# Moving the low-part splits of the weight units from GpSimd to VectorE, in the pairs stage of a two-block model kernel

## The reference, cut to what matters

```
r, k, v = split(conv3x3(h @ w_in[:, :3072]))             # context stream: 3-tap conv
w_log   = a_w0 + tanh(lora_w) @ a_w2;   iclr = sigmoid(a_a0 + lora_a @ a_a2)
decay   = exp(-exp(-softplus(-w_log) - 0.5))
kk      = k * a_k_k * rsqrt(sum_head((k * a_k_k)^2))
S <- S diag(decay) + (S a) b^T + v k^T,  y = S r         # per head, over tokens, both directions
```

## Time and profile before

| | |
|---|---|
| device time, 3 runs | 2478.40, 2481.42 (median), 2490.73 us |
| span of the profiled execution, first to last instruction | 2477.4 us (4.0 us under the median of the runs; its own time around the span is not given apart) |
| PE busy | 2412.3 us, 97% |
| DVE busy | 1255.9 us, 51% |
| ACT busy | 1190.7 us, 48% |
| POOL busy | 1353.1 us, 55%, nearly all in L171 |
| pairs stage | from about 170 to 888 us, some 85 us a pair |

### The profile page before, as it was taken

How to read it: one execution, slowest core, us unless ns; L and a number is a source line. 1 busy time by engine, 2 the same in 40 slices (tenths; PEclk the granted TensorE clock), 3 DMA queues, 4 the chain that set the end, 5 groups by cost and what they waited for, 6 DMA issues and landing times.

```text
span 2477.4 us, 60217 instructions
## 1 busy us (share of the span) xinstructions
PE 2412.3 (97%) x23314; PEld 2018.9 (81%) x23314; DVE 1255.9 (51%) x2368; ACT 1190.7 (48%) x1899; POOL 1353.1 (55%) x571
## 2 busy tenths in 40 slices
PE   6999999999999999999999999999999999999997
PEld 2278778777877878889999988888888888888886
DVE  5637776776677333245655445455344443333322
ACT  6533443444344334444444455555665555555554
POOL 0033211231122134437888887878777877777785
PEclk9989999999999999999999999999999999999999
DMA  8831211120111123326676654555455555555553
GB/s 344 309 109 62 70 47 48 56 70 30 56 62 64 47 78 102 100 97 212 236 254 236 238 186 165 175 170 176 164 167 173 186 169 178 169 178 169 170 181 133
DMA packets 100150, 361.40 MB, mean 146 GB/s; under 512 B 11120, under 2 KB 14320, under 8 KB 99728
## 3 DMA queue, kind: packets, MB, share of 16 engines
q1 hardware_dynamic: 99072, 357.90, 42.6%
q10 hardware_dynamic: 912, 1.03, 0.2%
HBM read 356.79 MB, written 2.10 MB: 145 GB/s over the span
## 4 chain that ended last, share of the span: by engine, by line
PE 93%; DVE 3%; ACT 2%; issue 1%; DMA 1%; SPq 0%; DVEq 0%; ACTq 0%
PE ps L207 26%; PE ps L208 13%; PE ps L180 6%; PE ps L181 6%; PE ps L182 6%; PE ps L633 6%; PE ps L634 4%; PE ps L635 4%; PE ps L813 2%; PE ps L803 1%; PE ps L827 1%; PE ps L881 1%; DMA W<-stream 1%; PE ps L848 1%; PE ps L711 1%
## 5 line engine op out<-in xcount | busy, mean ns | idle before, releaser
L171 POOL TENSOR_TENSOR wlo<-raw,whi 128x1024 fp32r<-128x1024 f32 x563 | 1349.6, 2411 | 1105.0 <-ACT whi L161 1066.4
L207 PE MATMUL ps<-acts,whi 128*128 128x512 f32 x2560 | 912.0, 401 | 1.4 <-DVE acts L2606 1.4
L161 ACT ACTIVATE whi<-raw 128x1024 fp32r<-128x1024 f32 x566 | 596.0, 1054 | 320.7 <-PE ps L208 136.7
L208 PE MATMUL ps<-acts,wlo 128*128 128x256 f32 x2560 | 714.9, 279 | 0.0
L207 PEld LDWEIGHTS ps<-acts,whi 128*128 128x128 f32 x2560 | 480.8, 188 | 114.0 <-DVE acts L2606 1.7
L208 PEld LDWEIGHTS ps<-acts,wlo 128*128 128x128 f32 x2560 | 482.6, 189 | 0.9
L180 PE MATMUL ps<-acts,whi 128*128 128x256 f32 (+1 forms) x1088 | 328.0, 301 | 0.0
L182 PE MATMUL ps<-acts,wlo 128*128 128x256 f32 (+1 forms) x1088 | 324.8, 299 | 0.0
L181 PE MATMUL ps<-acts,whi 128*128 128x256 f32 (+1 forms) x1088 | 324.8, 298 | 0.0
L633 PE MATMUL ps<-acts,whi 128*128 128x512 f32 (+1 forms) x576 | 224.0, 389 | 0.9 <-DVE W L1425 0.9
L180 PEld LDWEIGHTS ps<-acts,whi 128*128 128x128 f32 x1088 | 208.0, 191 | 8.3 <-POOL wlo L171 1.5
(11 more groups left out here) (361 smaller groups left out, 3343.4 us busy)
## 6 DMA issues: line engine op xcount, KB each, us to landing
raw<-stream SPq DMA_DIRECT2D x566, 512.0 KB, 3.3
W<-stream SPq DMA_DIRECT2D x64, 512.0 KB, 4.7
graw<-stream SPq DMA_DIRECT2D x32, 512.0 KB, 4.6
W<-xT SPq DMA_DIRECT2D x1, 4096.0 KB, 17.8
XR<-xT SPq DMA_DIRECT2D x16, 128.0 KB, 5.1
outT<-XR SPq DMA_DIRECT2D x4, 512.0 KB, 3.3
cns<-consts SPq DMA_DIRECT2D x1, 1056.0 KB, 5.1
cns<-consts SPq DMA_DIRECT2D x1, 896.0 KB, 7.3
```

Of the source, the lines that this page charges most:

```text
L161: nc.scalar.activation(whi[slot], raw[slot], ACT.Copy).then_inc(hi_done, 1)
L171: nc.gpsimd.tensor_tensor(wlo[slot], raw[slot], whi[slot].bitcast(F32), ALU.subtract).then_inc(lo_done, 1)
L207: nc.tensor.matmul(both_parts, whi[slot][:, k, :], hl[:, :, k0 + k, :], start=first and k == 0, stop=False)
L208: ins = nc.tensor.matmul(ps[:, bank, 0:T], wlo[slot][:, k, :], hl[:, 0, k0 + k, :], start=False, stop=last and k == UK - 1)
```

## The change

POOL's loop in the pairs stage goes; POOL only waits until the 67 units are done. In its place DVE has `dve_lo(dve, j, n)`, the same subtraction on the same tiles, at fixed places of its own list. Each of them first waits until ACT has made the high part (`hi_done`) and the ring place is free (`unit_used`). In a regular pair, units 5, 6, 7 stand in the scan, units 0, 1, 2 of the pair after it in the later part of the same scan, unit 3 in level 2 of the inverse and unit 4 at its end. At the start, DVE waits for POOL's last unit, then takes (0,3), (0,4), (0,5) ahead of `dve_decay(0)`, (0,6) ahead of the k convolution, (0,7) ahead of the r convolution and (1,0) ahead of `dve_norm_k(0)`; (1,1) and (1,2) stand ahead of `dve_rho(0)` in pair 0's inverse.

```diff
--- before.py
+++ after.py
@@ -1153,9 +1153,14 @@
             nc.gpsimd.memset(padk, 0.0).then_inc(R["pad_zero"].sem, 1)
             nc.gpsimd.memset(padr, 0.0).then_inc(R["pad_zero"].sem, 1)
             nc.gpsimd.memset(padc, 0.0).then_inc(R["pad_zero"].sem, 1)
-            with pool.Fori(0, PAIRS) as i:
-                for k in range(U_PAIR):
-                    split_lo(pool, (S_PAIR + k + LEAD) % RING, (i, U_PAIR, S_PAIR + k + LEAD))
+            pool.wait_ge(lo_done, pair_unit(PAIRS, LEAD))
+
+        def dve_lo(dve, j, n):
+
+            s = pair_unit(j, n)
+            dve.wait_ge(hi_done, s + 1)
+            dve.wait_ge(unit_used, s - (RING - 1))
+            nc.vector.tensor_tensor(wlo[s % RING], raw[s % RING], whi[s % RING].bitcast(F32), ALU.subtract).then_inc(lo_done, 1)
 
         def eight(v):
 
@@ -1368,6 +1373,8 @@
             if i:
                 dve_ydev(dve, i - 1)
             else:
+                dve_lo(dve, 1, 1)
+                dve_lo(dve, 1, 2)
                 dve_rho(dve, 0)
                 R["rho_ok"].wait(dve, 1)
                 R["dec_ok"].wait(dve, 3)
@@ -1391,6 +1398,8 @@
                         queried(0)
                     elif lv == 3:
                         go(conv_v, 2)
+                if lv == 2 and i + 1 < PAIRS:
+                    dve_lo(dve, i + 1, 3)
                 if lv == 4:
                     go(conv_v, 3)
                 elif lv == LEVELS:
@@ -1423,6 +1432,8 @@
                         dve_half(dve, i + 1)
             R["bonus_mm"].wait(dve, i + 1)
             nc.vector.tensor_tensor(bonp, ps[:, 0, 0:T], vc[:, 0:T], ALU.mult).then_inc(R["bonp_ok"].sem, 1)
+            if i + 1 < PAIRS:
+                dve_lo(dve, i + 1, 4)
 
         def dve_scan(dve, i):
 
@@ -1447,7 +1458,9 @@
             dve_keys(dve, j)
             state(1)
             dve_decay(dve, j)
+            dve_lo(dve, j, 5)
             state(2)
+            dve_lo(dve, j, 6)
             go(conv_r, 7)
             state(3)
             go(conv_r, 2)
@@ -1457,12 +1470,16 @@
             state(4)
             dve_keyed(dve, j)
             dve_keyed_ways(dve, j)
+            dve_lo(dve, j, 7)
             state(5)
             dve_alpha(dve, j)
             dve_scaled_keys(dve, j)
+            dve_lo(dve, j + 1, 0)
             state(6)
             dve_rho(dve, j)
             dve_bonus_in(dve, j)
+            dve_lo(dve, j + 1, 1)
+            dve_lo(dve, j + 1, 2)
             return conv_v
 
         def dve_pairs(dve):
@@ -1470,10 +1487,17 @@
             nc.vector.memset(kst_[:, 1:2], LN_EPS).then_inc(R["kconst"].sem, 1)
             nc.vector.memset(kst_[:, 2:3], 1.0).then_inc(R["kconst"].sem, 1)
             dve_half(dve, 0)
+            dve.wait_ge(lo_done, pair_unit(0, LEAD))
+            dve_lo(dve, 0, 3)
+            dve_lo(dve, 0, 4)
+            dve_lo(dve, 0, 5)
             dve_decay(dve, 0)
+            dve_lo(dve, 0, 6)
             go(dve_conv_k(dve, 0), 13)
             dve_keys(dve, 0)
+            dve_lo(dve, 0, 7)
             go(dve_conv_r(dve, 0), 10)
+            dve_lo(dve, 1, 0)
             dve_norm_k(dve, 0)
             dve_alpha(dve, 0)
             dve_beta(dve, 0)
```

## The result

| | kernel before | changed kernel |
|---|---|---|
| device time, median of 20 runs | 2482.93 us (2478.40 to 2490.73) | 2488.80 us (2483.63 to 2493.38) |
| ratio to before, 95% interval | 1 | 1.0025 [1.0017, 1.0033] |
| span of the profiled execution | 2477.4 us | 2486.8 us |
| DVE busy | 1255.9 us | 1233.7 us |
| POOL busy | 1353.1 us | 1199.4 us |

The change makes the kernel 5.9 us slower, 0.25%; forecast were 3.8 us and 2485.2 us. In a second comparison the same kernel came out at 1.0040 [1.0027, 1.0053]. So the loss is real and small.

The account below looks back on a forecast made before the run. PE was taken to bound the kernel, DVE having time to spare. Regular pairs -1.3, start +2.7 and inverse +2.4 summed to +3.8 us; on the median of 2481.4 that gave 2485.2 us, range 2476 to 2493.

Parts of the forecast that it names:

- What bounds: Pairs stage: PE sets the pace, busy 89.3 of 90 us; DVE's work costs time only where PE waits for it.
- Regular pairs, -1.3 us: Scans: DVE's stalls behind POOL go, so six PE gaps of 0.53 us become 0.31; the new subtractions cost nothing.
- third rival: PE's unexplained pauses amid small matmuls, 4.6 us together, fall into the new waits or go: 2480.6 us, chance 0.18.
- The start, +2.7 us: Pair 0's start: subtraction ahead of the decay delays ACT 4.45 us, PE waits 2.6, first square comes 2.7 us later.
- The inverse, +2.4 us: Pair 0's inverse: two subtractions ahead of dve_rho delay the key mask; PE's second half of the keys comes 2.4 us later.
- The clock: Second rival: PE's new waits near 190, 211 and 222 us lower its clock; one fall gives 2492 us, chance 0.07.
- signs of being wrong: Late state or L1404 each pair, clock 0.50 after 170 us, first square before 211, or pairs shorter by over 0.3 us.
- thin stretch of rows 10: Kernel before: PE busy 1.1 of 3.7 us, then granted clock 0.50 for 13.7 us; each new gap was called shorter.
- The 4.0 us that the prediction put between span and median: Whole kernel: the runs' median was taken to lie 4.0 us above the profiled span of 2477.4, at 2481.4 us.
- A late subtraction in every pair: First rival: subtractions at the two narrow places come late in each of 7 pairs, 17 us, 2502 us, chance 0.10.
- the narrow place: Unit 5 behind dve_decay in the scan: a 1.21 us subtraction put into a 1.32 us wait, 0.1 to spare.
- a clearly faster kernel: Fourth rival: DVE's stalls set PE's pace after all in the regular pairs; 17 us less, 2464 us, chance 0.05.

Follow-up runs that it names:

- e7: Changed kernel with every DVE subtraction from unit 3 of pair 1 on made twice; 1.0040 of the kernel before.
- e2: Only the start of the change: DVE subtracts up to unit 2 of pair 1, POOL the rest as before; 1.0036 of the kernel before.
- e9: The reordered start of e3, with POOL subtracting from unit 3 of pair 1 on as in the kernel before; 0.9981 of the kernel before.
- e1: Only the regular part of the change: POOL subtracts up to unit 2 of pair 1, DVE from unit 3 on; 1.0008 of the kernel before.
- e3: Changed kernel with the subtractions of the start and of pair 0's inverse moved to where DVE would wait anyway; 0.9989 of the kernel before.
- e4: Changed kernel with 5, 4 and 4 unused matmuls on PE ahead of pad_k, first square and key mask waits in pair 0; 1.0015 of the kernel before.
- e5: Changed kernel with only the part ahead of pair 0's inverse reordered as in e3; 1.0004 of the kernel before.
- e6: Changed kernel with only pair 0's inverse reordered as in e3; 1.0013 of the kernel before.
- e8: Changed kernel with 2 unused matmuls on PE in each of the three waits of pair 0; 1.0013 of the kernel before.
- e10: The changed kernel once more, unaltered, on the chip of e9; 1.0040 of the kernel before.

## Why the prediction was right, and where it was not

**What bounds.** That PE sets the pace in the regular pairs held: e7 adds 9.7 us of DVE to each pair for 0.4 us, its clock fall included.

**Regular pairs, -1.3 us.** The mechanism and the size held: the 0.53 us gaps are gone, and two undisturbed pairs run in 83.90 us where the kernel before has 84.11 and 84.13, 0.22 us a pair. Even so the changed kernel takes 507.84 us from pair 1 to pair 7 and the one before 506.67. What ate the gain are the pauses of my third rival, in which PE waits for nothing shown: they grew instead of shrinking. The chain of the changed kernel has 1.56 us of "issue" at 304.74, which is not there before. I compared each distance between two starts of PE with the median of the same two lines in all traces and added up what is over it by more than 0.18 us, leaving out what every pair of every kernel has:

```
pair 1 to pair 7, us                   total   late DVE  pauses   rest
before                                 506.67   1.30      1.64   503.7
changed                                507.84   none      4.08   503.8
e2, e9 (POOL in the regular pairs)     508.08, 507.91   1.38, 1.30   3.14, 2.88   503.6, 503.7
e1, e3, e4, e5, e6, e8, e10 (DVE)      505.79 to 508.95   none   1.74 to 4.93   503.8 to 504.1
```

The gap ahead of PE's step is there in all three kernels in which POOL subtracts, and in none in which DVE makes one subtraction per unit. The pauses differ by more than this gain, from 1.6 to 4.9 us, with no order by who subtracts, and hide it. (The prediction counts six such gaps; there is a seventh in pair 0's scan, at 286.2 us, 0.2 us more.)

**The start, +2.7 us.** 42.01 - 39.45 = +2.56 us without the clock's part (e8). The steps are where they were forecast: `act_exp_neg` at 190.08 (189.8), PE's wait 2.4 us idle and 2.7 from start to start (2.6). e5 and e3 show it from the other side.

**The inverse, +2.4 us.** 13.24 - 10.84 = +2.40 us.

**The clock.** This is the step that failed: the sum has no term for it, and a granted clock of 0.50 after 170 us, one of the signs of being wrong, is there. The rival had the place right, and with 0.07 a chance far too small: it argued that each gap was shorter than the thin stretch of rows 10 and that a wait of 2 us had cost nothing, and took 2.6 us for the same case. In the traces no fall stands behind the seven waits of 2.2 to 2.3 us (from start to start, ahead of the first square, in before, changed, e1, e2, e6, e7 and e10), and one behind each of the ten of 2.5 to 2.7 us (two each in changed, e2, e7 and e10, one each in e5 and e6). Its price of 6.9 us was taken from a fall of 13.7 us; the falls were 3.4 and 6.8 and cost 4.2 together.

**The sum.** In the profiled executions the changed kernel takes 8.05 us more up to pair 7's square: 4.0 up to the first square (2.6 and the clock's 1.5), 2.4 up to the keys, 0.45 up to pair 1 and 1.2 from there. The 0.45 are 2.7 for the clock less 2.2 that went, nearly all of it three things that the kernel before has and the changed one has not: pauses of 0.60 and 1.24 us in pair 0's inverse (at 226.2 and 230.0) and the seventh gap of 0.2. The 1.2 are 2.4 of longer pauses less the 1.3 of the six gaps, to 0.1. So the pauses gave back in one part what they took in another, which is luck. From the first to the last instruction the two executions differ by 9.4 us, more than the medians' 5.9. All other executions have 2.1 to 2.3 us around their span; by this the profiled one of before took an estimated 2479.6 us, 3.3 below the median of its 20 runs, and that of the changed kernel, with 2488.95, lies at its median. The 4.0 us that the prediction put between span and median were thus in part due to that one execution. The forecast of +3.8 us came near 5.9 because its two large terms were right. That 2488.8 lies within its range, to 2493, is due to the room for this rival: the clock's 4.2 us had been left out of the sum and taken into the range.

**The other rivals.** A late subtraction in every pair did not happen (0.58 us idle behind the narrow place), nor did a clearly faster kernel. The third rival came true in pair 0's inverse alone, where the pauses went, and the reverse came true behind it.

## What to carry to other kernels

Read the start of a stage by itself: the engine with 26 us to spare in each regular pair was the path there, and one instruction put ahead of `dve_decay(0)` held ACT up by over 4 us. When work is moved to an engine that runs its list in order, put it where that engine waits already, and check each place against what the next instruction on it releases. And price a new wait of PE not only by its length: here the two waits of 2.7 and 2.6 us cost 1.5 and 2.7 us more in clock.

## What the runs showed of the hardware that I had not expected

**The clock after short waits.** At waits of PE of 2.5 to 2.7 us the granted clock was 0.5 for 3.4 or 6.8 us; with 1.7 us of unused matmuls in the same waits it stayed at 1.00 (e8). The length of a wait does not decide alone. A third fall in e7, at 545 us, came behind a pause of 1.80 us amid small matmuls, and falls in e1, e4 and e7 at 866 to 877 us came behind pauses of 1.72 to 1.75 us. Pauses of the same 1.75 us in e3 (860.6) and e5 (863.0) and of 2.05 us in e5 (296.6) brought none. What decides between these the runs do not show.

**Pauses of PE amid small matmuls.** Between two matmuls, with nothing to wait for, PE pauses for 0.3 to 2.1 us from start to start (2.5 once, in e8), often at the same places in several traces but with other lengths. The chain of the changed kernel has, as its longest between pair 1 and pair 7,

```profile
304.74 1.56 issue
```

and the DMA view of 303 to 305.5 us has one packet on the queue that carries instructions:

```profile
q8 instruction: 1, 0.02, 2.4%
```

Over the stage that queue has a packet every 6.7 us in the mean. I counted the pauses between two matmuls of one line in all twelve traces, leaving out 0.32 us at L818 that is there in every pair. All 73 begin within 2.4 us behind the start of such a packet, a stretch that covers about a third of the time. That speaks for PE waiting for its own instructions. It was not tested, and why a kernel with the same PE program has longer or shorter ones stays open; they are what limits this comparison to some 3 us.
